# Two bursts of four products in place of one burst of eight, in a gather loop on one core

## What is computed

```python
q = (xb @ wq).reshape(PEER_BLOCK, PEER_HEADS, 2, PEER_HALF)
s = jnp.einsum('thpd,hpkd->thpk', q, subkeys)
sv, si = lax.top_k(s, PEER_TOPK)
...
top_v, top_i = lax.top_k(cand, PEER_TOPK)
expert = jnp.take_along_axis(cand_id, top_i, axis=-1)
gate = jax.nn.softmax(top_v.astype(jnp.float32), axis=-1).astype(xb.dtype)
act = jax.nn.gelu(jnp.einsum('thkd,td->thk', u_tab[expert], xb))
return jnp.einsum('thk,thkd->td', gate * act, v_tab[expert])
```

## Time and profile before

| | us |
|---|---|
| three runs, median (lowest to highest) | 4258.13 (4247.56 to 4258.9) |
| the profiled execution | 4242.17 |
| its span, first to last instruction | 4240.4 |
| TensorE matmul busy in it | 3207.4 (76%) |
| VectorE busy | 2485.9 (59%) |
| GpSimd busy | 1622.4 (38%) |
| ScalarE busy | 793.6 (19%) |

### The profile page before, as it was taken

One profiled execution on the slowest core, in us unless ns is written; L12 is line 12 of the kernel. 1 busy time (PEld: TensorE's weight loads), 2 busy tenths in 40 slices (PEclk: granted clock), 3 DMA queues, 4 the chain that ended last, 5 costly groups with the idle time before them and its releaser, 6 DMA issues. The chain is left out here.

```text
span 4240.4 us, 46656 instructions
## 1 busy us (share of the span) xinstructions
PE 3207.4 (76%) x15717; PEld 1723.2 (41%) x15717; DVE 2485.9 (59%) x7746; ACT 793.6 (19%) x1291; POOL 1622.4 (38%) x1372
## 2 busy tenths in 40 slices
PE   6999987875698877877788777777666676666676
PEld 4898876764265542521255343243111111111111
DVE  2553553238854656777765656677776555555554
ACT  4233322342123222210123112111000000000000
POOL 2101104434365644542355544353333333333332
PEclk9999998977799987977899888798666666666666
DMA  5001106534899999998999999999999999999998
GB/s 219 32 31 62 52 22 217 202 104 155 331 373 395 392 407 367 375 377 346 371 402 411 390 393 405 383 402 366 369 395 388 414 409 405 412 413 404 413 414 338
DMA packets 224168, 1352.42 MB, mean 319 GB/s; under 512 B 28631, under 2 KB 38167, under 8 KB 81726
## 3 DMA queue, kind: packets, MB, share of 16 engines
q0 software_dynamic: 156672, 1140.92, 66.7%
q1 hardware_dynamic: 67262, 208.51, 13.4%
HBM read 1319.52 MB, written 29.81 MB: 318 GB/s over the span
## 5 line engine op out<-in xcount | busy, mean ns | idle before, releaser
L1117 DVE CUSTOM_DVE_ANT_0 peer_uv<-peer_uv,all_PS 128x512 f32<-128x512 f32 x2176 | 1435.4, 685 | 1108.9 <-PE all_PS L1055 561.8
L1038 POOL DMA_INDIRECT peer_uv<-in_uv,peer_idx x1088 | 1039.1, 955 | 1485.4 <-PE all_PS L1075 1170.6
L1055 PE MATMUL all_PS<-peer_hT,peer_sel 96*128 96x512 bf16 x2176 | 979.1, 466 | 816.6 <-DVE peer_halves L1117 765.5
L1055 PEld LDWEIGHTS all_PS<-peer_hT,peer_sel 96*128 96x128 bf16 x2176 | 205.1, 101 | 1641.7 <-DVE peer_halves L1117 1273.1
L1075 PE MATMUL all_PS<-peer_uv,peer_zw 128*32 128x512 f32 x4352 | 843.9, 876 | 2.0 <-DVE peer_zw L1137 2.0
L921 POOL TENSOR_TENSOR flow_w_lo<-flow_w,flow_w_hi 128x1024 fp32r<-128x1024 f32 (+1 forms) x204 | 460.7, 2262 | 544.8 <-ACT flow_w_hi L914 544.4
L1091 ACT ACTIVATE peer_ge<-peer_pre 128x4 f32<-128x4 f32 x272 | 55.8, 205 | 2089.4 <-DVE peer_pre L1123 2089.3
L1075 PEld LDWEIGHTS all_PS<-peer_uv,peer_zw 128*32 128x32 f32 x4352 | 155.5, 143 | 433.4 <-issue 431.1
L941 PE MATMUL all_PS<-mix_h_hi,flow_w_hi 128*128 128x384 f32 (+1 forms) x672 | 283.8, 422 | 37.1 <-POOL flow_w_lo L921 31.9
L914 ACT ACTIVATE flow_w_hi<-flow_w 128x1024 fp32r<-128x1024 f32 (+1 forms) x204 | 203.6, 1004 | 339.5 <-PE all_PS L943 169.4
L942 PE MATMUL all_PS<-early_h_h_low,flow_w_hi 128*128 128x384 f32 (+1 forms) x672 | 226.2, 337 | 0.0
(11 more groups left out here) (307 smaller groups left out, 4627.8 us busy)
## 6 DMA issues: line engine op xcount, KB each, us to landing
flow_w<-in_w_gate_ab SPq DMA_DIRECT2D x48, 512.0 KB
flow_w<-in_w_query SPq DMA_DIRECT2D x48, 512.0 KB
flow_w<-in_w_conv SPq DMA_DIRECT2D x36, 512.0 KB
peer_uv<-in_uv,peer_idx POOLq DMA_INDIRECT x1088, 10.9
peer_uv<-in_w_ada SPq DMA_DIRECT2D x8, 2048.0 KB, 8.6
stream_heads_w<-in_w_heads SPq DMA_DIRECT2D x24, 512.0 KB, 4.9
flow_w<-in_w_proj_b SPq DMA_DIRECT2D x24, 512.0 KB
flow_w<-in_w_out SPq DMA_DIRECT2D x24, 512.0 KB
```

Of the source, the lines that this page charges most:

```text
L1038: self.nc.gpsimd.indirect_dma_start(out=self.uv[:, n % self.NUV, :], out_offset=None, in_=self.A["uv"], in_offset=bass.IndirectOffsetOnAxi ...
L1055: nc.tensor.matmul(PS[:, f, :], self.sel[:, c:c + 1].broadcast_to([3 * GR, P]), self.hT[:, g % self.NH, f * 512:(f + 1) * 512], start=True ...
L1117: nc.vector.tensor_tensor_reduce(part, part, PS[:, f, :], 1.0, 0.0, ALU.mult, ALU.add, self.halves[:, d, f, e:e + 1]).then_inc(M["dotted"], 1)
```

## The change

In `spread`, the condition no longer asks for f == 1, and one half of the sum is issued each time it holds: after the first half spread of a token n with n % 4 == 1 the four products of e = 0, after the second the four of e = 1. Where dense products stand between the two half spreads, they now stand between the two bursts as well. The two bursts of the very last group are issued as before.

```diff
@@ -1054,9 +1054,8 @@
                 pe.wait_ge(M["dotted"], s - 1)
             nc.tensor.matmul(PS[:, f, :], self.sel[:, c:c + 1].broadcast_to([3 * GR, P]), self.hT[:, g % self.NH, f * 512:(f + 1) * 512],
                              start=True, stop=True).then_inc(M["h_spread"], 1)
-            if n >= BT and f == 1 and n % BT == 1:
-                for e in range(2):
-                    self.summed(pe, n // BT - 1, e)
+            if n >= BT and n % BT == 1:
+                self.summed(pe, n // BT - 1, f)
         if self.at["pe"] == 2 * T and upto >= T:
             for e in range(2):
                 self.summed(pe, T // BT - 1, e)
```

## The result

The changed kernel takes 4287.32 us, median of five runs (4280.12 to 4292.62), the kernel before on the same chip 4256.01 (4243.11 to 4258.9). The ratio is 1.0082, 95% interval 1.0064 to 1.0101: **slower by 35 us** (27 to 43). The profiled execution took 4282.69 us, 41 more than the one of before.

A forecast was written before the change was run, and what follows sets the result against it. The transfers (gathers and weight stream) were taken as the bound. 11 of VectorE's 29 us plus 1 us of TensorE made 12 us, so the median was forecast at 4258 + 12 = 4270 us, range 4249 to 4287.

The forecast's parts named there:

- The tail: Last part of the loop: the new order ends at the same instant, S + 4.80, and the period stays 9.97 us.
- rival E: Tail held by the loop from last product to gather to dot, switches hide: 12 us faster or slightly more; chance 0.08.
- second switch: TensorE beside dense products: entering a second burst costs 0.22 us a group, 24 us in all, 1 us taken as passing.
- C: Rival: the second switch costs 0.22 us or more a group beside dense products, TensorE the bound; price 24 us, chance 0.08.
- The mechanism on VectorE: Token 4k+1's second half dot starts 1.79 us later, delaying a phase's work behind it: 1.8 us, or 2.15, per long step.
- The count: 18 long steps between tokens 4k+1 and 4k+2, in choosing, keys and norm, where VectorE is late.
- The direction: Whole kernel: slower 0.39, faster 0.08, same 0.53.
- I take two parts in five: Of VectorE's 29 us of delay at long steps, 11 us pass to the kernel's time; bounds 0 and 29.
- rival D: VectorE's 29 us pass nearly whole, every delay falling where the queue has run dry: 25 to 29 us; chance 0.15.
- queue of ten buffers: Where the DMA engines are full, VectorE's delay is lost in the queue of up to ten buffers.
- the dips: Some ten DMA dips where delay passes whole; share there to be lower by about 0.1 to 0.2 at long steps.
- Cost nothing: TensorE's wait for `weighed`, now ahead of spread 1 and dense products, costs nothing, as spread 0 covers it.

The follow-up runs named there:

- the kernel split only at the ends: Kernel before, bursts split only at the 32 groups of first tokens, norm, keys and pick where a step ends right behind token 4k+1: 1.0052, +22 us.
- the wait alone: Kernel before with only a wait for the weights added behind the first half spread, no product moved: 1.0015, +6 us.
- the dense-only kernel: Kernel before, bursts split only where the spreads are issued between dense products: 1.0025, +10.6 us; run again 1.0017, +7 us.
- 15 others: Kernel before, all eight products issued one token later at 15 groups where a step ends behind token 4k+2: 0.9963, 16 us faster.

## Why the prediction failed

**Right.** The tail: same last product, period 9.98, no change in 1000 us (rival E falls). TensorE's second switch: 0.22 us a group, hidden (C falls). The mechanism on VectorE and its size at one step, 1.69 and 2.10 us against 1.8 and 2.15. The count, too: 9 long steps in pick, 7 in keys and 2 in norm are what the trace has. The direction was given 0.39.

**Wrong, the step "I take two parts in five".** Of the 29 us of VectorE 11 were to pass. The terms, each as forecast and as the lag grew at these steps in the trace: pick in the third block (the second in the forecast's words) 9 and 8.7, in the one before it 9 and 8.5, norm 2 and 2.5, keys 9 and 5.7. The delays of keys were made up within the phase. Those of norm and pick passed whole: with the first tokens (below) they make 23 us at the steps, the three kernels that are split there are 19 to 25 us longer in these phases, and the kernel split only at the ends is 22 us (17 to 28) slower. That is nearly rival D. The argument was that a delay is lost in the queue of ten buffers, and passes only in the dips. But the lag is kept: 34.52 us before the step shown, 36.21 right behind it, 36.49 ahead of the next, 38.17 behind it. Of the 38.44 us that it reaches at token 668 it loses 0.5 in the next six tokens, far less than three parts in five. The queue of ten buffers does not supply the slack that the text had it supply.

**Wrong, a term left out.** The first 24 tokens also run beside steps of the choosing, and two long ones stand behind a token 4k+1, 1.69 us each: 3.4 us that no sum had.

**Wrong, "Cost nothing" for the wait that moves.** It was read from one group of the tail, where the weights are ready 0.5 us early. The text named the case without that cover, ScalarE late and dense products queued behind, and gave it no price. In the dense phases ScalarE waits for weight tiles, and 17 times the cover was gone: 6 us for the wait alone, 7 to 11 with the split beside dense products. No range had this term.

**The sum as measured:** step ends 22, beside dense products 9 (mean of 10.6 and 7.2), together 31 of 35 (27 to 43). The other 4 us are inside the intervals; whether the two parts add something to each other is open.

Also wrong: the dips were to be deeper by 0.1 to 0.2 and are not. What falls is the mean from 1300 to 3100 us (0.97 to 0.95, and 0.97 again in the second profile of the kernel before). Also, 446 tokens were put beside dense products, 111 groups; the dense-only kernel splits 103.

## What to carry to other kernels

When work is moved ahead on an in-order engine, list every wait that moves with it and what comes to stand behind it, and look up the cover of that wait in each phase, not in the cleanest one: here it was there in the tail and gone in the dense phases. When two engines hand work to each other, put the long burst of the one under the long work of the other; a split that makes the hand-over late costs as much as the right place gains (+22 us from 32 places, -16 us from 15 others). Before a delay is said to be absorbed, follow the lag of one item over the next few groups and to the end of the phase: in pick it stayed and passed, in keys it was gone.

## What I had not expected of the hardware

A 0.16 us operation on 128x4 elements took 2.31 us on VectorE (2498.95, above) while GpSimd made a low half of weights in 2.34 us:

```profile
2498.90 2.34 POOL L921 TENSOR_TENSOR flow_w_lo<-flow_w,flow_w_hi 128x1024 fp32r<-128x1024 f32 x1 [11.17 <-ACT flow_w_hi L914]
```

Of the 272 such operations in the kernel before 14 take over 0.4 us, 25 us in all, and all 14 overlap such an operation of GpSimd and end 0.02 to 0.04 us after it, as if each had waited for its end. Eight more overlap one and take the usual 0.16 us; these start within 0.12 us of GpSimd's start. Each slow one that TensorE is waiting for lengthens the wait for the weights. The other way round, GpSimd's issue of a gather took 1.77 us in place of 0.94 (3148.38, above) beside a 1.23 us bf16 operation of VectorE; in the first tokens, norm and pick together 14 issues take over 1.2 us after and 6 before. That the two engines hinder each other there is what the overlaps suggest; no run separates it.
